# Moving the normalised rows' two buffers 32 bytes further on in each partition

## The reference

```python
# first network
memn = rms_norm(mem, mem_norm_g)
n = rms_norm(h, mix_norm_g[i]);  proj = n @ w_in[i]          # s5 branch, gated branch, two gates
h = h + (gate_a * (ya @ w_proj_a[i]) + gate_b * (yb @ w_proj_b[i])) @ w_out[i]
h = h + memory_cross_attention(rms_norm(h, xattn_norm_g[i]), memn, w_q[i], w_k[i], w_v[i], w_xo[i])
h = h + swiglu(rms_norm(h, ffn_norm_g[i]), w_gate[i], w_up[i], w_down[i])
# second network, two layers, on x and on a context; n is the normed and modulated row
parts = split(n @ w_in)        # fourier, conv, two attentions, four gates
y = sum(gates * ys) @ w_out
h = h + swiglu_2(n, w1, w3, w2)     # (silu(n @ w1) * (n @ w3)) @ w2
```

## The kernel before

| buffer | size, bytes | start modulo 512, from `w_high` |
|---|---|---|
| `w_high`, `w_rest` | 32768, 16384 | 0 |
| `ahead_of_n` (pad) | 192 | 0 |
| `n_high`, `n_rest` (and `n_mem`, `n_x`, under the same bytes) | 8192 each | 192 |
| `behind_n` (pad; its first 17 words hold `q_scale` and `rope_sign`) | 832 | 192 |
| `hx`/`hx_r`, `hc`/`hc_r`, `kv_r` | 8192, 8192, 22528 | 0 |
| `hid_high`, `hid_rest`, `b_high`, `b_rest`, `work_r` | 22528, 22528, 4096, 4096, 36864 | 192 |

## Time and profile before

### The profile page before, as it was taken

One profiled execution on the slowest core, in us unless ns is written; L12 is line 12 of the kernel. 1 busy time (PEld: TensorE's weight loads), 2 busy tenths in 40 slices (PEclk: granted clock), 3 DMA queues, 4 the chain that ended last, 5 costly groups with the idle time before them and its releaser, 6 DMA issues.

```text
span 2240.8 us, 41517 instructions
## 1 busy us (share of the span) xinstructions
PE 2110.9 (94%) x17009; PEld 1980.6 (88%) x17009; DVE 1603.8 (72%) x2112; ACT 1011.5 (45%) x1207; POOL 297.3 (13%) x291
## 2 busy tenths in 40 slices
PE   7899999899889999999999889999999988999998
PEld 6675898799789999999999878999999987899998
DVE  7987667688687755555679877785557997776554
ACT  4112546544554533444444465453345446544332
POOL 3772004100100100100201210120010121000000
PEclk9999999999999999999999999999999999999999
DMA  8688766665335555565566422556555542345652
GB/s 255 229 283 314 249 231 217 220 195 174 113 102 169 182 186 188 184 191 188 190 186 193 135 76 94 172 172 197 189 177 178 180 140 88 101 132 156 198 192 75
DMA packets 292260, 397.42 MB, mean 177 GB/s; under 512 B 9270, under 2 KB 257292, under 8 KB 285452
## 3 DMA queue, kind: packets, MB, share of 16 engines
q1 hardware_dynamic: 285620, 383.53, 52.4%
q0 software_dynamic: 3008, 5.56, 1.1%
q10 hardware_dynamic: 3480, 6.18, 0.8%
HBM read 387.53 MB, written 3.15 MB: 174 GB/s over the span
## 4 chain that ended last, share of the span: by engine, by line
PE 76%; DVE 15%; ACT 4%; issue 3%; DMA 2%; POOL 0%; DVEq 0%; SPq 0%; ACTq 0%; POOLq 0%
PE L L937 62%; DVE w_rest L452 3%; PE M L937 3%; PE L L1211 2%; PE L L1197 2%; ACT w_high L446 1%; PE M L1465 1%; DVE work L2814 1%; DVE m L2129 1%; PE L L1224 1%; DMA raw<-in_w_ada 1%; PE L L1280 1%; DMA gate<-in_mem 1%; DVE n_rest L2138 1%; PE M L1071 1%
## 5 line engine op out<-in xcount | busy, mean ns | idle before, releaser
L937 PE MATMUL L<-n_high,w_high 128*128 128x256 f32 x3104 | 877.1, 283 | 12.6 <-DVE n_rest L2138 4.9
L937 PE MATMUL L<-n_rest,w_high 128*128 128x256 f32 x3104 | 866.8, 279 | 0.0
L937 PE MATMUL L<-n_high,w_rest 128*128 128x256 f32 x3104 | 866.6, 279 | 0.0
L452 DVE TENSOR_TENSOR w_rest<-raw,w_high 128x2048 fp32r<-128x2048 f32 x293 | 673.7, 2301 | 198.1 <-PE L L937 188.5
L446 ACT ACTIVATE w_high<-raw 128x2048 fp32r<-128x2048 f32 x293 | 561.1, 1916 | 335.8 <-PE L L937 297.7
L937 PEld LDWEIGHTS L<-n_high,w_high 128*128 128x128 f32 x3104 | 590.1, 190 | 30.7 <-issue 21.2
L937 PEld LDWEIGHTS L<-n_rest,w_high 128*128 128x128 f32 x3104 | 588.7, 190 | 0.0
L937 PEld LDWEIGHTS L<-n_high,w_rest 128*128 128x128 f32 x3104 | 588.4, 190 | 0.0
L937 PE MATMUL L<-hid_high,w_high 128*128 128x256 f32 x768 | 215.1, 280 | 4.2 <-DVEq L2612 4.2
L937 PE MATMUL L<-hid_high,w_rest 128*128 128x256 f32 x768 | 214.3, 279 | 0.0
L937 PE MATMUL L<-hid_rest,w_high 128*128 128x256 f32 x704 | 196.5, 279 | 0.0
(11 more groups left out here) (422 smaller groups left out, 2974.4 us busy)
## 6 DMA issues: line engine op xcount, KB each, us to landing
raw<-in_w_in SPq DMA_DIRECT2D x116, 1024.0 KB, 5.5
raw<-in_w_ffn SPq DMA_DIRECT2D x99, 1024.0 KB, 5.3
raw<-in_w_ada SPq DMA_DIRECT2D x32, 1024.0 KB, 6.2
raw<-in_w_out SPq DMA_DIRECT2D x16, 1024.0 KB, 4.9
raw<-in_w_gate SPq DMA_DIRECT2D x11, 1024.0 KB, 5.3
raw<-in_w_up SPq DMA_DIRECT2D x11, 1024.0 KB, 5.3
raw<-in_w_down SPq DMA_DIRECT2D x11, 1024.0 KB, 4.9
work<-in_w_ada SPq DMA_DIRECT2D x8, 1024.0 KB, 7.3
```

The costliest lines, as they stand in the source:

```text
L452: nc.vector.tensor_tensor(w_rest[:, u.first % 2, :], raw[:, u.first % 4, :], w_high[:, u.first % 4, :].bitcast(F32), ALU.subtract).then_in ...
L937: ins = mm(dst, a, b, start=first and i == 0, stop=last and i == 2, skip_group_check=skip)
```

## The change

The pad ahead of the normalised rows grows by eight words and the pad behind them shrinks by eight. `n_high` and `n_rest` (and `n_mem`, `n_x`, `q_scale` and `rope_sign`, which share these bytes or the pad) start 32 bytes further on in each partition: at 224 instead of 192 in the table's count. Every other buffer stays where it is. The instructions of all five engines, their order and their waits are the same as before; only these addresses in them differ.

```diff
-        ahead_of_n = sb("ahead_of_n", [P, 48])
+        ahead_of_n = sb("ahead_of_n", [P, 56])
         over = ExitStack()
         with over:
             n_mem = over.enter_context(nc.sbuf_tensor("n_mem", [P, DC, T], F32))
             n_x = over.enter_context(nc.sbuf_tensor("n_x", [P, DC, T], F32))
         n_high = sb("n_high", [P, DC, T], F32R)
         n_rest = sb("n_rest", [P, DC, T], F32R)
-        behind_n = sb("behind_n", [P, 208])
+        behind_n = sb("behind_n", [P, 200])
```

## The result

The changed kernel takes 2271.26 us (median of 4 runs, 2267.69 to 2274.04), the kernel before 2247.39 us (median of 4, 2242.23 to 2248.26). The ratio is 1.0118, 95% interval 1.0096 to 1.0140: slower, as forecast, and 2 us from the 2269 us of the prediction. The profiled execution took 2274.04 us with a span of 2272.2 us, 31.4 us more than the span before.

A forecast was written before the change was run, and what follows sets the result against it. TensorE, busy 94% of the span with 62% of the chain in line 937's matmuls, was taken as the bound. Profiled 2242.55 us plus 27 for normalised-row matmuls gave 2269 us; likeliest 2258 to 2276, 8 in 10 2222 to 2290.

The forecast's parts named there:

- 0.86 in the sum: Share of the 9312 normalised-row matmuls taken to lie on the chain, from 62% of the span in line 937.
- the quick rhythm: Faster of two start-to-start paces in dense stretches of line 937's matmuls: 113.3 ns, against 117.8 ns for the slower.
- The sum's term of 27 us: Matmuls moving `n_high` or `n_rest` all at 117.8 ns: 6984 x 4.4 ns x 0.86, 27 us more.
- such a piece: 64 bytes of a partition, 16 columns of a moved chunk; the change's 32 bytes are half, making 113.3 ns unreachable.
- The extra of 6.7 ns: Per matmul, the 113.3 ns pace over the columns' 106.7 ns, read as the time of 16 columns, 64 bytes.
- The lock: After a pause TensorE's moving columns and weight load fall into 113.3 or 117.8 ns and keep it 50 to 120 us.
- The reading that half clock takes no more than the columns: At half clock, matmuls 212 ns apart take no more than 256 columns at 1.2 GHz, 213.3 ns, with no choice of pace.
- Small terms: 384 matmuls on standing `n_high` under 1 us; 544 float32 ones given nothing, at most 3.6 us; VectorE 479, ScalarE 498 ns unchanged.
- The spread: Run times, two of them 6 us above the profiled one, should spread less once `n_high` blocks stop choosing a pace.
- Slower still: Rival: a chunk off the 64-byte multiple needs 17 pieces for 16, 120.0 ns per matmul, +45 us, 2287 us; chance 0.18.
- Nothing happens: Rival: only the rhythm a pause leaves decides, blocks draw anew whatever the address: 2242 to 2248 us; chance 0.21.
- Faster: Rival: distance 224 ends the slow rhythm, 9 us less, 2234 us, or towards 2180; chance 0.24 mildly, 0.10 by more.

The follow-up runs named there:

- weights_too: From the kernel before, both weight buffers and the normalised rows 32 bytes further on, hidden, branch and work rows unmoved: 2259.67 us, ratio 1.0061.
- plus64: From the kernel before, the normalised rows 64 bytes further on, at 256 from the weights: 2286.78 us, ratio 1.0187.
- scan: Bare kernel of matmul bursts after pauses, not the reference, moved operand 0 to 480 bytes from the standing one: 113.3 or 117.8 ns at 192, 118.4 at 224.
- scan2: Bare burst kernel with 4-byte steps, separate high and rest distances, second standing operand shifted, other column counts: 113.3 ns at 192, 119.1 and 120.0 four bytes off.
- scan3: Bare burst kernel, 24 bursts per placement and two matmul orders: 113.3 ns in 13 of 24 at the kernel's placement, 24 with second standing operand 128 bytes on.

## Why the prediction was right

**What bounds it.** Right. The time went where the chain ran, into matmuls of line 937, and 0.85 of what TensorE gained in busy time reached the end, against 0.86 in the sum. That these agree is no test of how 0.86 was worked out: the chain's share of line 937 rose by three points (62% to 65%), where one was forecast, and VectorE's fell from 15% to 11%. More of the chain runs through TensorE now than the sum assumed.

**The pace at the new place.** Right in size, and only partly in its reason. The 2 us between 2269 and 2271.26 are partly luck: the sum stood on a profiled execution 5 us under the median of the kernel before, and its step of 27 us is 3 us over the 24 between the medians. All `n_high` blocks lost the quick rhythm. The new pace is 118.3 ns, which the trace of before did not have, and not the 117.8 that was taken as the nearest other. The sum's term of 27 us was 6984 x 4.4 ns x 0.86; by the counts it is 6145 x 5.0 and 2826 x 0.5 ns, times 0.86, 28 us, against 31.4 in the profiled spans and 24 in the medians. What the spans have beyond it did not come from other blocks' rhythms (514 of the work rows' 832 matmuls had the slower pace after, 320 before, which is under 1 us), but in the main from the float32 matmuls at half clock that the section on the result names.

**The reason given.** The step "moving one by half of such a piece can't make a better alignment than a whole multiple already is" led to the right sign but named the wrong thing. A place off the 64-byte multiple is harmless where the weights have it too (weights_too), and a place on the next multiple costs 43 us (plus64). What the prediction had read from the earlier trace rows, that the operands' distance goes with the pace, was the cause: it was shown with the moved buffer at one address and the weights at two (weights_too), and in the bare bursts. That 224 is among the slower places was in part luck: nothing in the trace of before told it from 448, which costs nothing. The extra of 6.7 ns as 64 bytes of a partition has nothing behind it in the runs.

**The lock.** The two rhythms are shown: the bare pattern has them after pauses, without any other engine's work beside it (scan). That they are a lock of the moving columns with the weight load is argued: the standing operand's width and place change the pace (scan2), but no run shows the two streams meet. What in a pause decides stays open; its length alone does not (scan3). The reading that half clock takes no more than the columns holds as a number, and leaves out that 128 moved columns take as long there (213.3 ns, scan2), so that it may be the load that takes the time.

**Small terms.** VectorE and ScalarE on the moved buffers: within 2 ns, 481 and 500 ns, as said. The 384 matmuls on standing `n_high` and the 544 float32 ones on `n_mem` and `n_x` cost under 1 us together.

**The spread.** The prediction expected it to shrink as the blocks stop drawing. It was 6.4 us over 4 runs, against 6.0 over 4 before; over 10 to 13 runs the kernel before spread by 10 to 15 us. Too few runs of the changed kernel to tell.

**The rivals.** "Slower still" has its pace, 120.0 ns and 2287 us, but at distances 0 and 256. "Nothing happens" is refuted by the ratio, and the rule behind it, from the Trainium skill, "TensorE: Matmul & The Clock Gate", section "Step-by-step: what each phase is for", that loading the next weights takes nothing from the running matmul, did not hold for the time of float32r matmuls at full clock: with the same 256 moved columns at distance 0, 64 standing columns in place of 128 took the pace from 120.0 to 113.3 ns (scan2), and with the moved operand at 224, the standing one 32 bytes on took it from 118.4 to 113.3 ns in three of four bursts (scan). "Faster" was wrong for 224; the quick rhythm for good exists, but by the rests' place.

## What to carry to other kernels

Where TensorE is full of matmuls, read their distance from start to start in several dense stretches, not their duration or the engine's busy share: two or three values that held for whole blocks went here with the distance of the two operands' addresses, and that can be changed with a pad. Try the placement in a bare burst kernel first, with several pauses for each place and all the operands of the pattern, since one operand in three at a bad distance was enough here, and with the same numbers of columns as the kernel, since 192 bytes were good for 256 moved columns and bad for 512. A pad of a few bytes was worth 1.2% one way and 0.7% the other, with no instruction changed.

## What was not expected of the hardware

- The pace of float32r matmuls (128 standing, 256 moved columns, full clock) depends on the operands' distance: 113.3 to 120.1 ns over 0 to 480 bytes, and 4 bytes off 192 cost the quick rhythm (119.1 and 120.0 ns). Places 256 bytes apart have the same paces. At half clock it is 213 ns.
- At 192 bytes a pause picks one of two paces, 113.3 or 117.8 ns, and it holds for a thousand matmuls.
- The second standing operand 128 bytes on took the draw away: 24 of 24 bursts at 113.3 ns, against 13 of 24.
- 128 moved columns took 111.7 ns a matmul, hardly less than 256, and at half clock 213.3, no less: loading 128 float32r columns seems to take as long as moving 256 (0.83 ns a column in the loads' records, an estimate of 107 ns).
